# Sparse attention in one program with its projections: queries ahead of gates, probabilities scaled on GpSimd, two weight quarters on VectorE

## The chip, the core and the metric

The kernel runs on one core of a Trainium2 chip. The core has five engines with a queue of their own each: TensorE (PE, matmuls), VectorE (DVE), ScalarE (ACT), GpSimd (POOL) and SyncE (SP, which issues transfers). They run side by side and wait for each other by semaphores. The metric is the device time of one execution in microseconds (us); lower is better.

## What is computed

One inference step of a two-layer encoder for 1024 new frames ("prompt") and 32 frames of a running stream ("sample") with 512 cached positions. The first layer is a sparse attention, the second a gated linear recurrence; both have a SiLU gate and an output projection. The change is in the first layer:

```
p = rmsnorm(h) @ w_in                  # split into q, k, v, z (gate), qi, ki, wi (indexer)
q, k, qi, ki = rope(q), rope(k), rope(qi), rope(ki)
score = sum_h wi[h] * relu(qi[h] @ ki.T)          # 8 indexer heads
sel = top_k(score, n_sel)                         # 256 keys (prompt), 136 (sample)
logits = q @ k[sel].T * ATT_SCALE                 # 8 heads of 128, 2 key heads
probs = softmax(logits)                           # admissible selected keys only
o = probs @ v[sel]
out = (o * silu(z)) @ w_out
```

Tokens are handled in 9 tiles: 0 to 7 are 128 prompt tokens each, tile t sees 128(t + 1) keys; tile 8 is the sample (32 tokens, 544 keys). Tiles 0 and 1 need no selection.

## The kernel before

The kernel is four programs ("blocks") one after the other, with a barrier of all engines between them: `norm_and_project` (line 259), `attention` (line 878), `out_and_recur` and `final_out`. Inside a program each engine works through a fixed list of instructions.

**Projecting** (`attention_project`). All tokens are kept transposed, in three parts of 352 columns. The weights come in tiles of 128 columns in the order of `TILES` (line 48): the indexer key, eight indexer queries, two keys, then for each head the gate tile (Z) and the query tile (Q). A tile and a part make a "unit": 24 matmuls on TensorE (`product`, line 187; each value is split into a high and a low half and three products are summed), then for a query unit three copies on ScalarE (lines 667 to 672), three operations on GpSimd (lines 721, 724, 710) which rotate it, and a store by SP to the DRAM tensor `q_rotated` (line 547); for a gate unit one SiLU on ScalarE (line 675). TensorE may be up to four units ahead of ScalarE, which reads the banks. Between the units the weights are split by ScalarE (line 209) and GpSimd (line 216), and rotated keys are turned into rows (`rows_before`) and stored.

**The threshold search** (`search`, `count_signs`). The selection is found by 31 steps of bisection on the bits of a threshold. In each step VectorE proposes a value (line 802), counts scores above it for five of the seven tiles (line 793), while ScalarE counts for the two largest (line 651); then VectorE decides (lines 808, 809). The search runs beside the last 48 units (gates and queries). ScalarE does step n after a unit chosen by `counted_after`: units are put down as 3850 ns each and a step as `PACE`, 6000 ns.

**Attending** (`attention`). 72 items, one for each tile and head. For item i: TensorE multiplies queries by keys (line 941) into one of two halves of the PSUM tensor `wide`; VectorE adds the mask and takes the minimum (`shift`, line 1027); ScalarE takes the exponential and its sum (line 1067); two items later VectorE takes the reciprocal (line 1035) and scales the probabilities (`divide`, line 1037); TensorE transposes them (line 954) four items behind the multiplication, ScalarE copies them out of the banks (line 1077), TensorE mixes the values in groups of four heads (line 970), and VectorE multiplies by the gate (line 1043). The probabilities have a ring of 5 buffers, in the space of the normalised rows. In tiles 1 to 7 VectorE also makes the mask of tile t + 1, one of eight marking operations (lines 1003 to 1017) in each item between `shift` and `divide`. The queries come back from DRAM tile by tile (`q_tile`, line 913). In items 48 and 56 ScalarE splits the high half of one quarter of the output weights (line 194); GpSimd makes the low half (line 201). The other two quarters' low halves are made by VectorE in the next program.

## Time and profile before

| | us |
|---|---|
| median of 3 runs | 1458.36 (1457.74 to 1459.96) |
| the profiled execution | 1460.28 |
| its span in the profile | 1458.5 |
| TensorE busy in the span | 1382.0 (95%) |
| VectorE busy | 927.7 (64%) |
| ScalarE busy | 640.3 (44%) |
| GpSimd busy | 553.8 (38%) |
| granted TensorE clock, mean | 0.982 of full speed |

The span is the time from the first instruction to the last in the profile of one execution. Busy time of TensorE is modelled and counts matmuls that wait in its pipeline, so 95% does not mean 95% of the peak. The busy shares are averages over stages that are limited by different engines; the stages by time are: normalising and first units to 260 us, gates and queries with the search from 260 to 442 us, attending from 457 to 650 us, output projection and recurrence, final output.

### The profile page before, as it was taken

The page shows a single profiled execution, that of the slowest core. Times are in us where ns is not written, and L with a number is a line of the kernel's source. Part 1 is how long each engine was busy: PE and PEld are TensorE (multiplying, and loading weights), DVE is VectorE, ACT ScalarE, POOL GpSimd, SP SyncE. Part 2 cuts the span into 40 slices and gives each one's busy share as a digit, 9 for nine tenths or more (in the row PEclk, how much of TensorE's full clock was granted, in tenths as well). Part 3 has the DMA queues.
Part 4 walks back from the last instruction along what each step waited for, and adds up shares of the span by engine and source line. Part 5 has one row for each costly group of instructions (what it writes and reads, how often), then busy time and mean ns, then how long its engine had stood idle before and what let it go on. Part 6 is the DMA issues. An engine that isn't in the chain of part 4 may idle for free. (4 is left out here: it accounts for less than half of the span.)

```text
span 1458.5 us, 21147 instructions
## 1 busy us (share of the span) xinstructions
PE 1382.0 (95%) x8028; PEld 1204.3 (83%) x8028; DVE 927.7 (64%) x1702; ACT 640.3 (44%) x1123; POOL 553.8 (38%) x399
## 2 busy tenths in 40 slices
PE   5999999999995899999998999999999999997998
PEld 5999845999993455548888999999999999996786
DVE  4211287878887988744557676767585858596233
ACT  4333365667765555541124534343443435343121
POOL 2466600455641001100023655556464737373000
PEclk9999999999997999999999999999999999998999
DMA  7221100223211400002221101111111111105221
GB/s 217 91 56 44 44 1 1 65 81 99 71 40 59 159 15 19 0 30 84 90 78 46 44 25 55 36 44 35 44 35 45 35 44 35 45 6 209 101 87 65
DMA packets 95315, 86.80 MB, mean 60 GB/s; under 512 B 5584, under 2 KB 83280, under 8 KB 95216
## 3 DMA queue, kind: packets, MB, share of 16 engines
q1 hardware_dynamic: 93584, 80.63, 18.0%
q0 software_dynamic: 1632, 4.82, 0.9%
q8 instruction: 66, 1.08, 0.3%
q14 instruction: 33, 0.27, 0.1%
HBM read 65.46 MB, written 19.97 MB: 59 GB/s over the span
## 5 line engine op out<-in xcount | busy, mean ns | idle before, releaser
L187 PE MATMUL bank<-hn_hi,rw_hi 128*128 128x352 f32 x768 | 251.7, 328 | 1.6 <-DVE hn_lo L177 1.6
L187 PE MATMUL bank<-hn_hi,rw_lo 128*128 128x352 f32 x768 | 247.9, 323 | 0.0
L187 PE MATMUL bank<-hn_lo,rw_hi 128*128 128x352 f32 x768 | 247.6, 322 | 0.0
L187 PE MATMUL bank<-hn_hi,w_hi 128*128 128x352 f32 x648 | 209.9, 324 | 0.0
L187 PE MATMUL bank<-hn_lo,w_hi 128*128 128x352 f32 x648 | 207.8, 321 | 0.0
L187 PE MATMUL bank<-hn_hi,w_lo 128*128 128x352 f32 x648 | 207.7, 321 | 0.0
L187 PEld LDWEIGHTS bank<-hn_hi,rw_hi 128*128 128x128 f32 x768 | 145.1, 189 | 3.5 <-issue 3.0
L187 PEld LDWEIGHTS bank<-hn_lo,rw_hi 128*128 128x128 f32 x768 | 145.6, 190 | 0.0
L187 PEld LDWEIGHTS bank<-hn_hi,rw_lo 128*128 128x128 f32 x768 | 145.2, 189 | 0.0
L721 POOL TENSOR_TENSOR swapped<-swapped,sin 128x352 f32<-128x352 f32 x57 | 54.0, 947 | 190.8 <-ACT swapped L668 125.8
L187 PEld LDWEIGHTS bank<-hn_hi,w_hi 128*128 128x128 f32 x648 | 121.6, 188 | 0.5 <-ACT relu L682 0.5
L187 PEld LDWEIGHTS bank<-hn_lo,w_hi 128*128 128x128 f32 x648 | 121.8, 188 | 0.0
L187 PEld LDWEIGHTS bank<-hn_hi,w_lo 128*128 128x128 f32 x648 | 121.5, 187 | 0.0
L793 DVE TENSOR_SCALAR_CACHE_REDUCE marks<-score,bits 128x384 bf16<-128x384 f32 (+5 forms) x157 | 117.1, 805 | 1.1
L240 POOL TENSOR_SCALAR stats<-stats 128x1 f32<-128x1 f32 (+1 forms) x27 | 6.5, 241 | 280.0 <-ACT junk L1242 152.0
L1273 POOL TENSOR_TENSOR rw_lo<-rw_raw,rw_hi 128x1024 fp32r<-128x1024 f32 x32 | 95.3, 2982 | 35.8 <-ACT rw_hi L1266 35.7
L1471 PE MATMUL wide<-levels 128*128 128x128 f32 (+1 forms) x832 | 98.0, 273 | 1.2 <-DVE last_state L1785 1.1
L1471 PEld LDWEIGHTS wide<-levels 128*128 128x128 f32 (+1 forms) x832 | 92.5, 185 | 6.7 <-issue 1.9
L1067 ACT ACTIVATE probs<-probs,low 128x128 f32<-128x128 f32 (+8 forms) x72 | 55.6, 772 | 88.3 <-DVE low L1027 87.8
L941 PE MATMUL wide<-kT,q_tile 128*128 128x512 f32 (+3 forms) x192 | 75.7, 508 | 14.8 <-DMA q_tile<-q_rotated 14.8
L1639 POOL TENSOR_TENSOR levels<-levels,k_rec 128x528 f32<-128x528 f32 (+1 forms) x48 | 89.0, 1878 | 1.4 <-ACT levels L1557 1.4
L1749 DVE TENSOR_TENSOR levels<-levels,q_rec 128x528 f32<-128x528 f32 (+1 forms) x48 | 87.4, 1886 | 0.0
(230 smaller groups left out, 2926.1 us busy)
## 6 DMA issues: line engine op xcount, KB each, us to landing
rw_raw<-in_rec_w_in SPq DMA_DIRECT2D x32, 512.0 KB, 4.0
w_raw<-in_att_w_in SPq DMA_DIRECT2D x27, 512.0 KB, 4.0
q_rotated<-relu SPq DMA_DIRECT2D x24, 176.0 KB, 1.9
xin<-in_x_prompt SPq DMA_DIRECT2D x8, 512.0 KB, 3.8
q_tile<-q_rotated SPq DMA_DIRECT2D x8, 512.0 KB, 3.9
wo_raw<-in_att_w_out SPq DMA_DIRECT2D x4, 1024.0 KB, 9.2
x_again<-in_x_prompt SPq DMA_DIRECT2D x8, 512.0 KB, 4.1
residual<-h_rows SPq DMA_DIRECT2D x8, 512.0 KB, 2.9
```

The costliest lines, as they stand in the source:

```text
L187: last = pe.matmul(out, l, r, start=n == 0, stop=n == len(passes) - 1)
L240: pool.tensor_scalar(stats[0:r, 1, t:t + 1], stats[0:r, 0, t:t + 1], 1.0 / D, EPS, ALU.mult, ALU.add).then_inc(pool_order, 1)
L721: pool.tensor_tensor(swapped[:, r % 3, :], swapped[:, r % 3, :], sin[:, part * CW:(part + 1) * CW], ALU.mult).then_inc(sin_done, 1)
L793: step(dve.tensor_scalar(marks[0:r, i % 2, 0:keys(t)], tile(i, t), bound, 0.0, op, ALU.add, accum_out=counts[0:r, first + i:first + i + 1]))
L941: last = pe.matmul(logits[0:rows(t), i % 2, a:e], q[:, t % 2, h, 0:rows(t)], src[:, h // GROUP, a:e], start=True, stop=True)
L1067: act.activation(probs[0:r, i % RING, 0:n], probs[0:r, i % RING, 0:n], ACT.Exp, scale=-1.0, bias=low[0:r, 0, i:i + 1], accum_out=low[0:r, ...
L1273: pool.tensor_tensor(S["rw_lo"][:, slot], S["rw_raw"][:, slot], S["rw_hi"][:, slot].bitcast(F32), ALU.subtract).then_inc(S["rec_lo_done"], 1)
L1471: last = pe.matmul(out[:, 0:r], left, right, start=True, stop=True)
L1639: pool.tensor_tensor(x, x, level_view(k[:, slot], m)[:, :, 0, :], ALU.mult).then_inc(k_scaled, 1)
L1749: dve.tensor_tensor(x, x, level_view(q[:, slot], m)[:, :, 1, :], ALU.mult).then_inc(q_scaled, 1)
```

## The change

- `TILES`: for each head the query tile comes ahead of the gate tile, so that the last three units are gates.
- `PACE` is 5000 instead of 6000.
- `norm_and_project` and `attention` become one program, `project_and_attend`, without a barrier between them. What the barrier did is done by waits: VectorE waits ahead of the first `shift` for the last unit read by ScalarE and the last stored rows; TensorE waits ahead of the first item for the key rows and the cache, and ahead of its first transpose for the banks.
- The queries of tiles 0 and 1 go to a space of their own, `q_first`, over the tables of cosines and sines, so that they can be loaded once the last query is stored. Tiles 2 and up use `q_tile` as before; tile 2 waits for the first item.
- GpSimd scales the probabilities. VectorE keeps the reciprocal.
- The low halves of the first two output weight quarters are made by VectorE, at i = 52 and i = 60 of its loop.

```
 for _i in range(HEADS):
-    TILES += [Z0 + P * _i, Q0 + P * _i]
+    TILES += [Q0 + P * _i, Z0 + P * _i]
...
+        S["q_first"] = Space(nc, space.at)("q_first", [P, 2, HEADS, P])
         S["cos"] = space("cos", [P, T])
...
-    BITS, PACE = 31, 6000
+    BITS, PACE = 31, 5000
...
             for t in range(NT):
-                if t >= 2:
+                if t == 2:
+                    sp.wait_ge(logits_ready, 1)
+                elif t >= 4:
                     sp.wait_ge(logits_ready, HEADS * (t - 1))
-                sp.dma_start(q[:, t % 2, :, 0:rows(t)],
-                             q_dram[:, :, span(t)].rearrange("h p t -> p h t")).then_inc(q_in[t % 2], 16)
+                sp.dma_start(queries(t)[:, :, 0:rows(t)],
+                             q_dram[:, :, span(t)].rearrange("h p t -> p h t")).then_inc(
+                                 q_in_first[t] if t < 2 else q_in[t % 2], 16)
...
+        def gpsimd(pool):
+            def divide(i):
+                t, h = items[i]
+                r, n = rows(t), keys(t)
+                pool.wait_ge(inv_done, i + 1)
+                pool.tensor_scalar(probs[0:r, i % RING, 0:n], probs[0:r, i % RING, 0:n], low[0:r, 2, i:i + 1], None,
+                                   ALU.mult).then_inc(probs_ready, 1)
+
             pool.tensor_copy(kTs[:, :, PAST:], kT[:, :, SEQ:T]).then_inc(keys_done, 1)
-            for c in range(2):
-                out_weights_lo(pool, S, c)
+            for i in range(N):
+                divide(i)
...
+            pe.wait_ge(S["k_rows_out"], NT)
+            pe.wait_ge(S["cache_out"], 3)
             for i in range(N + LAG + 4):
+                if i == LAG:
+                    pe.wait_ge(*S["units_read"])
+                    pe.wait_ge(*S["ropes_read"])
...
+            dve.wait_ge(S["open_done"], 3)
+            dve.wait_ge(*S["units_read"])
+            S["rows_stored"](dve)
             for i in range(N + 12):
...
                 if 2 <= i <= N + 1:
-                    divide(i - 2)
+                    t, h = items[i - 2]
+                    dve.wait_ge(exp_done, i - 1)
+                    dve.reciprocal(low[0:rows(t), 2, i - 2:i - 1], low[0:rows(t), 1, i - 2:i - 1]).then_inc(inv_done, 1)
+                if i in (6 * HEADS + 4, 7 * HEADS + 4):
+                    out_weights_lo(dve, S, i // HEADS - 6)
```

Three places show the order of instructions. The first is SP's queue at the hand-over from projecting to attending (`q_rotated<-relu` is a store of a rotated query part, `q_tile` and `q_first` are query loads). Before:

```order
L547 DMA q_rotated<-relu 128x352 [waits rope_done] x6
L267 UNCONDITIONAL_BRANCH [waits stored0,v_stored,stored1,q_stored1,q_stored0]
L908 UNCONDITIONAL_BRANCH [waits barrier_Pool_Activation_PE_DVE_SP_release]
L913 DMA q_tile<-q_rotated 128x8x128 x2
L913 DMA q_tile<-q_rotated 128x8x128 [waits logits_ready] x2
L918 DMA wo_raw<-in_att_w_out 128x4x512 x4
```

After:

```order
L547 DMA q_rotated<-relu 128x352 [waits rope_done] x5
L928 DMA q_first<-q_rotated 128x8x128 [waits q_stored1,q_stored0]
L928 DMA q_first<-q_rotated 128x8x128
L928 DMA q_tile<-q_rotated 128x8x128 [waits logits_ready]
L928 DMA q_tile<-q_rotated 128x8x128
L935 DMA wo_raw<-in_att_w_out 128x4x512 [waits logits_ready]
```

The first two query loads now wait for the stored queries alone.

The second place is VectorE's list in tile 1, two items (the operation on `wide` is `shift`, `marks` and `score` belong to a marking operation). Before:

```order
L1027 ISA probs,low<-wide,open_mask 128x256 [waits pT_ready,logits_ready]
L1027 ISA low 128x1
L1010 TENSOR_SCALAR marks,counts<-score,select_state 128x384
L1035 RECIPROCAL low<-low 128x1 [waits exp_done,mark_order]
L1037 TENSOR_SCALAR probs<-probs,low 128x128 [waits inv_done]
L1027 ISA probs,low<-wide,open_mask 128x256 [waits pT_ready,logits_ready]
L1027 ISA low 128x1
L1012 TENSOR_SCALAR marks<-score,select_state 128x384
L1035 RECIPROCAL low<-low 128x1 [waits exp_done,mark_order]
L1037 TENSOR_SCALAR probs<-probs,low 128x256 [waits inv_done]
```

After:

```order
L1055 ISA probs,low<-wide,open_mask 128x256 [waits pT_ready,logits_ready]
L1055 ISA low 128x1
L1038 TENSOR_SCALAR marks,counts<-score,select_state 128x384
L1080 RECIPROCAL low<-low 128x1 [waits exp_done,mark_order]
L1055 ISA probs,low<-wide,open_mask 128x256 [waits pT_ready,logits_ready]
L1055 ISA low 128x1
L1040 TENSOR_SCALAR marks<-score,select_state 128x384
L1080 RECIPROCAL low<-low 128x1 [waits exp_done,mark_order]
```

The scaling behind each reciprocal has left VectorE's list; the next `shift` stands directly behind the reciprocal.

The third place is GpSimd's list in the attention. Before:

```order
L923 COPY kT_sample<-kT 128x2x32
L201 TENSOR_TENSOR wo_lo<-wo_raw,wo_hi_85 128x4x512 [waits wo_hi] x2
```

After:

```order
L948 COPY kT_sample<-kT 128x2x32
L945 TENSOR_SCALAR probs<-probs,low 128x128 [waits inv_done] x8
L945 TENSOR_SCALAR probs<-probs,low 128x256 [waits inv_done] x8
L945 TENSOR_SCALAR probs<-probs,low 128x384 [waits inv_done] x8
L945 TENSOR_SCALAR probs<-probs,low 128x512 [waits inv_done] x8
L945 TENSOR_SCALAR probs<-probs,low 128x640 [waits inv_done] x8
```

The two weight operations have left GpSimd's list and 72 scalings have come in (the rows go on to 1024 keys and the sample).

## Rows read from the trace of the kernel before

**Rows 1.** The head of the page: the span of the profiled execution.

```profile
span 1458.5 us, 21147 instructions
```

**Rows 2.** Stretches: length; busy us of PE, PEld, DVE, ACT, POOL; granted clock; DMA.

```profile
259.20:441.80 182.60, 182.54 (x1155) 182.00 (x1154) 151.16 (x400) 128.35 (x236) 96.38 (x83) 1.00 0.24 68
441.80:457.30 15.50, 0.81 (x4) 0.81 (x4) 9.28 (x32) 4.90 (x8) 4.22 (x6) 0.59 0.34 102
...
462.40:475.10 12.70, 10.34 (x34) 5.51 (x33) 11.17 (x45) 6.65 (x27) 0.00 (x0) 0.87 0.21 58
475.10:489.90 14.80, 12.53 (x45) 6.28 (x45) 14.14 (x47) 8.14 (x25) 0.00 (x0) 1.00 0.94 336
489.90:507.00 17.10, 15.95 (x59) 8.44 (x59) 16.44 (x46) 9.69 (x25) 0.00 (x0) 1.00 0.08 21
507.00:528.40 21.40, 19.90 (x83) 11.86 (x84) 19.36 (x47) 12.14 (x29) 0.00 (x0) 1.00 0.11 31
528.40:553.20 24.80, 24.47 (x99) 13.92 (x98) 21.93 (x46) 13.76 (x32) 0.00 (x0) 1.00 0.09 26
553.20:584.20 31.00, 28.67 (x110) 15.65 (x109) 27.08 (x45) 17.27 (x33) 4.53 (x1) 1.00 0.04 6
584.20:616.80 32.60, 31.81 (x120) 16.77 (x118) 25.87 (x45) 18.30 (x32) 4.53 (x1) 1.00 0.00 0
```

**Rows 3.** Timelines of PE and DVE at the hand-over: start, length, instruction, [idle before].

```profile
441.42 0.32 PE L187 MATMUL bank<-hn_hi,w_lo 128*128 128x352 f32 x1
...
451.81 0.17 DVE L834 COPY_PREDICATED bits<-bits 128x7 uint32<-128x7 uint32 x1
...
456.50 3.17 PE L941 MATMUL wide<-kT,q_tile 128*128 128x128 f32 x10 [14.75 <-DMA q_tile<-q_rotated]
...
457.33 0.29 DVE L1027 CUSTOM_DVE_ANT_0 probs<-wide,open_mask 128x128 f32<-128x128 f32 x1 [5.35 <-PE wide L941]
```

**Rows 4.** Line 547, the last ten stores: issue ns min/median/max, first and last start.

```profile
L547 SPq DMA_DIRECT2D q_rotated<-relu x10: 319/320/345, 379.7 to 448.2; - x10
```

**Rows 5.** The page's DMA issues: KB each, us from issue to landing.

```profile
q_rotated<-relu SPq DMA_DIRECT2D x24, 176.0 KB, 1.9
...
q_tile<-q_rotated SPq DMA_DIRECT2D x8, 512.0 KB, 3.9
```

**Rows 6.** Timeline of DVE, the start of two steps of the search.

```profile
263.22 0.16 DVE L802 TENSOR_SCALAR bits<-bits 128x7 uint32<-128x7 uint32 x1
...
267.63 0.17 DVE L802 TENSOR_SCALAR bits<-bits 128x7 uint32<-128x7 uint32 x1
```

**Rows 7.** Groups by line, 263 to 452 us: busy us, mean ns, idle before.

```profile
L808 DVE TENSOR_TENSOR bits<-counts,select_state 128x7 uint32<-128x7 f32 x31 | 14.4, 466 | 28.6 <-ACT signs L651 28.0
...
L809 DVE COPY_PREDICATED bits<-bits 128x7 uint32<-128x7 uint32 x31 | 12.6, 407 | 1.1
...
L802 DVE TENSOR_SCALAR bits<-bits 128x7 uint32<-128x7 uint32 x31 | 11.1, 358 | 1.0
```

**Rows 8.** Groups by line and form on DVE, 455 to 652 us.

```profile
L1037 DVE TENSOR_SCALAR probs<-probs,low 128x1024 f32<-128x1024 f32 x8 | 6.0, 753 | 0.3
...
L1027 DVE CUSTOM_DVE_ANT_0 probs<-wide,score 128x384 f32<-128x384 f32 x8 | 4.4, 549 | 0.0
...
L1037 DVE TENSOR_SCALAR probs<-probs,low 128x384 f32<-128x384 f32 x8 | 3.4, 420 | 0.3
```

**Rows 9.** Lines 1615 (GpSimd) and 201 (VectorE): duration ns min/median/max.

```profile
L1615 POOL TENSOR_SCALAR k_rec<-k_rec x8: 1063/1067/1103, 782.3 to 1257.8; 128x1056 f32<-128x1056 f32 x8
...
L201 DVE TENSOR_TENSOR wo_lo<-wo_raw,wo_hi x2: 2282/2286/2291, 653.2 to 655.4; 128x2048 fp32r<-128x2048 f32 x2
```

**Rows 10.** Timelines of POOL and DVE around the second weight quarter.

```profile
589.45 4.53 POOL L201 TENSOR_TENSOR wo_lo<-wo_raw,wo_hi 128x2048 fp32r<-128x2048 f32 x1 [26.86 <-ACT wo_hi L194]
...
590.57 3.90 DVE L1037 TENSOR_SCALAR probs<-probs,low 128x896 f32<-128x896 f32 x1
594.39 1.21 DVE L1027 CUSTOM_DVE_ANT_0 probs<-wide,score 128x1024 f32<-128x1024 f32 x1
```

More of the change, by code:

```diff
@@ L155, in build @@
         S["tables_in"], S["cache_in"] = sem("tables_in"), sem("cache_in")
-        norm_and_project(nc, S, space)
-        attention(nc, S)
+        project_and_attend(nc, S, space)
         out_and_recur(nc, S)
@@ L256, in cached_keys, with project_and_attend @@
     return score[:, 0:PAST // P * 384].rearrange("p (b c) -> p b c", b=PAST // P)
-def norm_and_project(nc, S, space):
+def project_and_attend(nc, S, space):
     swapped = space("swapped", [P, 3, CW])
@@ L265, in norm_and_project @@
     S["swapped"], S["relu"] = swapped, relu
-    first, later = input_norm(nc, S), attention_project(nc, S)
+    stages = [input_norm(nc, S), attention_project(nc, S), attention(nc, S)]
     with nc.Block() as block:
@@ L269, in _ @@
         def _(sp):
-            first["sync"](sp)
-            later["sync"](sp)
+            for stage in stages:
+                stage["sync"](sp)
         @block.tensor
         def _(pe):
-            first["tensor"](pe)
-            later["tensor"](pe)
+            for stage in stages:
+                stage["tensor"](pe)
         @block.scalar
         def _(act):
-            first["scalar"](act)
-            later["scalar"](act)
+            for stage in stages:
+                stage["scalar"](act)
         @block.gpsimd
         def _(pool):
-            first["gpsimd"](pool)
-            later["gpsimd"](pool)
+            for stage in stages:
+                stage["gpsimd"](pool)
         @block.vector
         def _(dve):
-            first["vector"](dve)
-            later["vector"](dve)
+            for stage in stages:
+                stage["vector"](dve)
 def input_norm(nc, S):
@@ L940, in multiply @@
                     e = min(n, a + 512)
-                    last = pe.matmul(logits[0:rows(t), i % 2, a:e], q[:, t % 2, h, 0:rows(t)],
+                    last = pe.matmul(logits[0:rows(t), i % 2, a:e], queries(t)[:, h, 0:rows(t)],
                                      src[:, h // GROUP, a:e], start=True, stop=True)
@@ L1029, in shift @@
                                          op1=ALU.min, accum_out=low[0:r, 0, i:i + 1]).then_inc(logits_read, 1)
-            def divide(i):
-                t, h = items[i]
-                r, n = rows(t), keys(t)
-                dve.wait_ge(exp_done, i + 1)
-                dve.reciprocal(low[0:r, 2, i:i + 1], low[0:r, 1, i:i + 1]).then_inc(inv_done, 1)
-                dve.wait_ge(inv_done, i + 1)
-                dve.tensor_scalar(probs[0:r, i % RING, 0:n], probs[0:r, i % RING, 0:n], low[0:r, 2, i:i + 1], None,
-                                  ALU.mult).then_inc(probs_ready, 1)
             def gate(g):
@@ L1055, in _, with scalar @@
                 if 2 <= i <= N + 1:
-                    divide(i - 2)
+                    t, h = items[i - 2]
[3 more added lines that the diff above has]
+                    out_weights_lo(dve, S, i // HEADS - 6)
                 if i >= 12 and i % 4 == 0:
                     gate((i - 12) // 4)
-        @block.scalar
-        def _(act):
+        def scalar(act):
             for i in range(N + LAG):
@@ L1082, in _ @@
                     out_weights_hi(act, S, i // HEADS - 6)
+    return dict(sync=sync, tensor=tensor, scalar=scalar, gpsimd=gpsimd, vector=vector)
 def out_and_recur(nc, S):
```

40 lines of the change are left out of this document (24 added, 16 removed).

## The prediction

> **What bounds the kernel now.** I read the page's head first: the profiled execution spans 1458.5 us [rows 1] and the run it belongs to took 1460.28 us, so 1.8 us lie around the span; the median of the runs shown is 1458.36 us. I take the saving off the span and then off the median. The page's chain of waits covers only the last 110 us and says nothing about the stage that is changed, so I went on to the table of stretches [rows 2], cut where the first score read (line 1027) of each query tile starts. It shows four regimes. Until 441.8 us TensorE is busy 182.54 of 182.60 us: the projections are bound by TensorE. Then follows a hole of 15.5 us in which TensorE does 0.81 us of work. In tiles 1 to 3 (462.4 to 507.0) VectorE is the busier engine: 14.14 of 14.80 us in tile 2, 16.44 of 17.10 in tile 3, against 12.53 and 15.95 for TensorE, whose figure is generous because it counts the overlapping ends of matmuls. From tile 7 on TensorE is the bound again, 31.81 of 32.60 us. So the change can win in two places: the hole, and the tiles in which VectorE is the slower one. Everything after 650 us is the same code, behind the same barrier.
>
> **The hand-over, part by part.** The hole before has three members in series [rows 3]. The last projection matmul ends at 441.42 + 0.32 = 441.7 (call it T). VectorE ends the threshold search only at 451.81 + 0.17 = 452.0. Then comes the barrier between the two programs, then the query load, and TensorE's first score matmul starts at 456.50, its reader on VectorE at 457.33. T to that reader is 15.6 us. The change acts on each member.
>
> The search: 31 steps, and step n must be answered by ScalarE, which does its share at fixed places among its 48 last projection units. Before, a step is scheduled every 6.0 us of units, after, every 5.0 us. A step takes VectorE 267.63 - 263.22 = 4.4 us undisturbed [rows 6]. The three small operations that close and open it are held at times: their means are 0.466, 0.407 and 0.358 us against 0.17 undisturbed [rows 7], 0.30 + 0.24 + 0.19 = 0.7 us a step. So VectorE needs 5.1 us a step, 31 x 5.1 = 158 us, and from 263.2 it could be through at 421. With some waiting left I take 430, 12 us before T. The search then no longer ends last.
>
> What is late next is the query load. The stores of the rotated queries must land before SP may load them. Before, the last query unit is also the last unit: its store is issued at 448.2 [rows 4], 6.5 us after T, and lands 1.9 us later [rows 5], at T + 8.4. After, three gate units stand behind it; 182.6 us over 48 units are 3.8 us each, 11.4 us in all. The store lands at T - 3.0, the load is issued at once and takes 3.9 us [rows 5]: queries at T + 0.9. From first matmul to first reader were 0.83 us [rows 3] at a granted clock of 0.59; I take 0.7. First reader at T + 1.6 instead of T + 15.6: **14.0 us saved**. The bounds: if the two loads delay each other and ScalarE is late with its first exponential, 12; if the queries are there in time and only the last gate holds VectorE, 15. Moving queries ahead of gates costs nothing in the projections themselves: the same 48 units in another order, and TensorE has no gap there whose cover could go. SP's queue is moved too: the two loads now stand behind the last row stores of the keys, which are some 17 units earlier, and the next two tile loads wait for the first score, since their space is that of the normalised rows.
>
> **The scaling on GpSimd.** Removed from VectorE are 72 operations at line 1037, 0.42 us for 384 keys and 0.753 for 1024 [rows 8]; the next operation starts 0.08 us before such a one ends (594.39 against 590.57 + 3.90 in [rows 10]), so the relief is 0.34 us at 384 keys and 0.067 us more or less for each 128: 0.27, 0.34 and 0.41 us an item in tiles 1, 2 and 3, or 2.2, 2.7 and 3.3 us a tile of 8. The trace has no such operation on GpSimd. The nearest row is its one-source multiply-add over 128x1056, 1.067 us [rows 9], about 1.0 ns an element: 0.4, 0.5 and 0.6 us for these tiles, and 1.1 us at 1024, four times less than the 4.1 us an item that tile 7 takes. The upper bound is its two-source subtraction, 4.53 us for 2048 elements [rows 10], 2.3 us at 1024; even that fits. I take the one-source row, since the new operation reads one tensor and a scalar. GpSimd is otherwise empty here (one operation of 4.53 us in each of tiles 6 and 7 [rows 2]). The result is needed two items later, so its own length and one semaphore hop more are hidden by that distance.
>
> What is not hidden is that the two engines get in each other's way. While GpSimd runs its subtraction from 589.45 to 593.98, a scaling of 896 keys on VectorE, which needs less than the 0.753 us of 1024, lasts 3.90 us and ends 0.5 us behind it [rows 8, 10]. So VectorE's marking operations (one an item in tiles 1 to 7) may be held by a scaling that GpSimd is still doing. Between the reciprocal that starts the scaling and the marking operation stands the score read, 0.549 us at 384 keys [rows 8], one source of it in PSUM, against about 0.5 us of scaling, plus the start: 0.1 us is left over an item, 0.8 us a tile. The bounds are nothing, and the whole scaling (0.5 us an item, 4 us a tile), if the score read is held too. The Trainium skill, "GPSIMD Engine Reference", 1. Specifications, says that the SBUF interfaces are shared with VectorE, with contention from VectorE instructions in a 2-port mode or with two SBUF inputs; the score read is neither. By that rule the small end holds, and the trace agrees in the one 3.90 us row. The same page, 4.1 Engine selection, speaks against the change: GpSimd is about half as fast for two-input elementwise work, and roughly at line rate for one input.
>
> Tile by tile. TensorE's own work in a tile's stretch goes by 2t + 1 (scores of tile t, half the transposes of t and of t - 1, mixing of t - 1), so from 31.8 us in tile 7 [rows 2] it is 2.12 x (2t + 1): 6.4, 10.6, 14.8, 19.1, 23.3 and 27.6 us in tiles 1 to 6. Before, against these: 12.7, 14.8, 17.1, 21.4, 24.8, 31.0. After:
> tile 1: 12.7 - 2.2 + 0.6 = 11.1 (VectorE); tile 2: 14.8 - 2.7 + 0.8 = 12.9 (VectorE); tile 3: VectorE 17.1 - 3.3 + 0.8 = 14.6, TensorE 14.8, and two equal bounds do not mesh, 16.0; tile 4: 19.1 plus 1.0 for the same reason, 20.1; tile 5: 24.2; tiles 7 and 8 as now, tile 0 too (it goes by ScalarE's exponentials as much as by VectorE). That is 1.6 + 1.9 + 1.1 + 1.3 + 0.6 = 6.5 us.
>
> **The two weight quarters.** In tile 6 TensorE loses 31.0 - 27.6 = 3.4 us, the most of all tiles; there GpSimd's first quarter holds VectorE, and a second one does so in tile 7 [rows 10]. They go to VectorE at 2.286 us each [rows 9], into items whose VectorE sum leaves about 1.2 us free. Each thus makes one score read late by 1 to 2 us, of which TensorE feels about half. Held 3.2 us twice before, late 1 to 2 us twice after: 1.9 us saved, between -1 and 3.5.
>
> **Sum.** 14.0 + 6.5 + 1.9 = 22.4 us. Span 1458.5 - 22.4 = 1436.1; against the median, 1458.4 - 22.4 = **1436 us**.
>
> **The rivals.** (A) GpSimd holds VectorE for the whole scaling in every item. Then in tiles 1 to 3 the relief of 8.2 us is paid back with 3.2, 4.0 and 4.8 us, tiles 4 to 6 stay as they are, and only the hand-over is won: 1458.4 - 14.0 + 3.8 = 1448, or 1443 if half of the items are held. For it: the 3.90 us row. Against it: the score read between. Chance 0.12. (B) The coupling of three engines costs more today than I allow, and after the change every tile goes at its own bound: 6.4 does not bind in tile 1 (VectorE 10.5), but 12.1, 14.8, 19.1, 23.3 and 27.6 do. That is 2.2 + 2.7 + 2.3 + 2.3 + 1.5 + 3.4 = 14.4 us in the stage instead of 8.4, 1430, and with the better end of the hand-over 1429. Chance 0.12. (C) The other side: the faster schedule of the search. ScalarE takes its units in order; if a step cannot keep to 5.0 us, ScalarE falls behind and, three units (11.4 us) behind, TensorE stands still in a stretch where it has no idle time at all. Behind by 4 + 31 x (s - 4.96) for steps of s; it cancels 22.4 us at 34 us behind, s = 5.9. Today a step lasts 188.8 / 31 = 6.1 us; were that inherent, 38 us behind, 27 us lost: 1463. Against it: my 5.1 us are 1.0 below today's, and the rest is waiting for the slow schedule. ScalarE is busy 128.35 of 182.6 us [rows 2], so it has room for the denser counts; stepping through the first 33 units with these lengths I found it at most 7 us behind. Chance 0.04. (D) The hand-over fails in part: the query chain (stores, then loads) takes 6 to 10 us longer than counted, or the change does not move the search ahead: 1442 to 1450. Chance 0.06.
>
> **How the numbers follow.** Forecast 0.66 (1432 to 1441), A 0.12, B 0.12, C 0.04, D 0.06. The range must take in B's 1429 and most of A, so 1429 to 1446; it leaves out C, half of D and the worse end of A, some 0.15. A measurement of this kernel can tell about 0.2% (2.9 us) from no change; only C reaches there, with a sliver of D: faster 0.95, same 0.02, slower 0.03.
>
> **What would show it.** In the profile after, the last bit operation of the search should end near 430, before the last projection matmul; TensorE's hole should be about 1 us and wait for the query load; the new GpSimd operations should measure about 1.0 ns an element; a marking operation should show 0.1 us of holding, not 0.5; tile 1 should take 11 us and tile 6 29. ScalarE's counts should start behind their units by single microseconds. I am wrong if TensorE has gaps before the hand-over (C), if the stage from first score read to last gate is still above 190 us (A), or below 180 (B).

## The result, and the profile after

| | before | after |
|---|---|---|
| median, us | 1458.85 (4 runs, 1457.74 to 1459.96) | 1448.12 (4 runs, 1446.90 to 1449.22) |
| ratio after / before | | 0.9926, 95% interval 0.9914 to 0.9938 |
| profiled execution, its span | 1460.28, 1458.5 | 1447.48, 1445.6 |

The change makes the kernel 10.7 us faster, not 22.4; 1448.1 is above the range's upper end of 1446. One run among all those below, 2304.02 us at a granted clock of 0.56 (PACE 5500 with early additions), is left out. In the profiled executions the spans differ by 12.9 us, and that can be laid out by place: the first score read comes at 450.6 instead of 457.3 (6.7 us), from there to the last gate of the sample ("the stage" below) it takes 187.0 instead of 192.4 us (5.4 us), and the rest 808.0 instead of 808.8. So the hand-over gave half of the 14.0 that it should, and the stage 5.4 of 8.4.

The stretches of after, with the columns of [rows 2]. The first is the hole at the hand-over, then come tiles 1 to 7 and the sample:

```profile
445.85:450.60 4.75, 0.99 (x5) 0.93 (x4) 0.00 (x1) 1.75 (x2) 0.00 (x0) 0.73 0.83 221
...
455.83:466.48 10.65, 8.03 (x32) 4.27 (x31) 9.37 (x36) 6.43 (x26) 6.14 (x8) 1.00 0.06 8
466.48:479.10 12.62, 12.06 (x44) 5.95 (x44) 11.54 (x38) 8.02 (x26) 9.23 (x10) 1.00 0.89 331
479.10:495.60 16.50, 16.30 (x61) 8.62 (x62) 14.05 (x38) 9.87 (x26) 11.50 (x8) 1.00 0.12 34
495.60:516.42 20.82, 20.14 (x85) 11.86 (x84) 15.63 (x38) 12.20 (x29) 15.52 (x9) 1.00 0.15 42
516.42:540.78 24.36, 24.36 (x98) 13.92 (x97) 18.36 (x38) 13.76 (x32) 16.22 (x9) 1.00 0.09 26
540.78:571.30 30.52, 28.61 (x110) 15.70 (x109) 22.16 (x38) 17.26 (x33) 21.87 (x9) 1.00 0.03 6
571.30:602.99 31.69, 31.66 (x120) 16.66 (x118) 19.01 (x37) 18.27 (x32) 23.33 (x9) 1.00 0.00 1
...
602.99:637.62 34.63, 33.31 (x152) 17.12 (x152) 8.64 (x30) 13.42 (x42) 20.66 (x11) 0.97 0.01 1
```

Three things are to be seen. VectorE is no longer the busier engine in tiles 2 and 3 (14.05 of 16.50 us in tile 3, before 16.44 of 17.10); in tile 1 it still is, 9.37 of 10.65 us against TensorE's 8.03. The fifth busy column, GpSimd, was to be near 5 us in tile 3 and is 11.50; in tile 7 it is 23.33. And tile 6 has hardly moved (30.52 against 31.0), while the sample, 33.0 us long before (616.8 to the last gate at 649.7), has become longer.

The hand-over, timelines of TensorE, VectorE, ScalarE, GpSimd and SP with the columns of [rows 3]:

```profile
415.84 0.43 PE L187 MATMUL bank<-hn_hi,w_hi 128*128 128x352 f32 x1 [0.86 <-ACT relu L676]
...
421.63 0.43 PE L187 MATMUL bank<-hn_hi,w_hi 128*128 128x352 f32 x1 [1.67 <-ACT relu L676]
...
426.54 0.43 PE L187 MATMUL bank<-hn_hi,w_hi 128*128 128x352 f32 x1 [0.79 <-ACT qiT_zT_gT L679]
...
436.27 0.64 DVE L838 COPY_PREDICATED bits<-bits 128x7 uint32<-128x7 uint32 x1
...
439.42 0.45 ACT L676 COPY relu<-bank 128x352 f32<-128x352 f32 x1 [4.03 <-DMA q_rotated<-relu]
...
441.76 1.84 POOL L714 TENSOR_TENSOR relu<-relu,swapped 128x352 f32<-128x352 f32 x2
...
445.54 1.00 SPq L928 DMA_DIRECT2D q_first<-q_rotated  x2
...
445.57 0.32 PE L187 MATMUL bank<-hn_hi,w_lo 128*128 128x352 f32 x1
...
449.65 2.53 PE L965 MATMUL wide<-kT,q_first 128*128 128x128 f32 x8 [3.76 <-DMA q_first<-q_rotated]
...
450.60 0.29 DVE L1055 CUSTOM_DVE_ANT_0 probs<-wide,open_mask 128x128 f32<-128x128 f32 x1 [13.69 <-PE wide L965]
```

The search is indeed out of the way (436.9). But TensorE, which before had no gap there, now waits three times for ScalarE, and T, the end of the last projection matmul, is at 445.9 instead of 441.7. The queries are rotated and stored late as well, so that their loads start at 445.5 and TensorE waits 3.76 us for them. The 14.0 us saved were reckoned from T to the first reader, 15.6 down to 1.6. It is 450.60 - 445.89 = 4.7, and T itself has slipped by 4.2: 15.6 - 4.7 - 4.2 = 6.7.

### The profile page after: what moved, and what is told of

The parts are those of the page before. It is cut to its first block and busy times, and to the rows that moved or that the text cites. A ratio compares the mean times of both kernels' runs of the same rounds, so it can differ in the third digit from the quotient of the medians.

```text
span 1445.6 us, 21141 instructions
## 1 busy us (share of the span) xinstructions
PE 1380.3 (95%) x8028; PEld 1202.4 (83%) x8028; DVE 904.1 (63%) x1632; ACT 641.2 (44%) x1123; POOL 674.3 (47%) x469
## 5 line engine op out<-in xcount | busy, mean ns | idle before, releaser
L945 POOL TENSOR_SCALAR probs<-probs,low 128x128 f32<-128x128 f32 (+8 forms) x72 | 127.7, 1778 | 62.8 <-DVE low L1080 62.6
```

The costliest lines, as they stand in the source:

```text
L945: pool.tensor_scalar(probs[0:r, i % RING, 0:n], probs[0:r, i % RING, 0:n], low[0:r, 2, i:i + 1], None, ALU.mult).then_inc(probs_ready, 1)
```

## Theory and rivals

My theory after the traces had three parts. (1) The hand-over lost 7.3 us because PACE 5000 asks for a search step every 5.0 us and VectorE needs 5.5, so that ScalarE, which answers the steps in order with its units, comes late. That is rival C's mechanism at a fraction of its size. The rivals: it is the order of the units, or the joined program. (2) GpSimd's scaling is 2.5 times slower than its own multiply-add, by the pointer operand or by the one-operation form, or because VectorE is in its way. (3) The weight quarters cost time on VectorE, by where they stand or wherever they stand.

The experiments ran on three chips. Each was compared with runs of the kernel before on its own chip, whose medians were 1462.0 us (the runs with gates first, PACE 5500, VectorE's scaling, a constant), 1459.8 us (PACE 6000, early additions, two operations, quarters one item earlier) and 1458.2 us (the others). So the ratios, not the times, compare the experiments with each other and with the 0.9926 of the changed kernel; where the intervals of two ratios overlap, the argument rests on the stretches of the profiled executions.

## Experiments on the hand-over

**Gates ahead of queries again**, all else as changed.

```
-    TILES += [Q0 + P * _i, Z0 + P * _i]
+    TILES += [Z0 + P * _i, Q0 + P * _i]
```

> The changed kernel with the gate tile ahead of the query tile again. Theory (the order takes 11.4 us of the query chain out of the hand-over): the last store is issued 6.5 us behind the last projection matmul, queries arrive 10 to 11 us behind it, first score read near 453 to 456; total 3 to 6 us above 1448. Rival (the order brings nothing, since ScalarE and GpSimd are late with the last query tile either way): total within 1 us.

Measured: 1457.72 us (1455.47 to 1459.29), ratio 0.9970 (0.9958 to 0.9982); the first read is at 457.72, where it was before the change at 457.33 [rows 3], and later than the 453 to 456 that I expected: the order is worth more than I thought.

```profile
452.67 1.00 SPq L928 DMA_DIRECT2D q_first<-q_rotated  x2
...
456.77 3.36 PE L965 MATMUL wide<-kT,q_first 128*128 128x128 f32 x10 [12.41 <-DMA q_first<-q_rotated]
```

The search ends at 438.0 here and does not matter: stores and loads of the queries alone fill the whole hole. Joining the programs and hurrying the search bring nothing at all at the hand-over without the new order. What is left of the gain is the stage.

**Order and pace alone**, in the kernel before: two programs, old place of the queries, scaling and quarters as before. The edit is against the kernel before.

```
-    TILES += [Z0 + P * _i, Q0 + P * _i]
+    TILES += [Q0 + P * _i, Z0 + P * _i]
-    BITS, PACE = 31, 6000
+    BITS, PACE = 31, 5500
```

> The kernel before with only two numbers changed: queries ahead of gates, and PACE 5500. The two programs stay apart, the barrier and the old place of the queries stay, scaling and quarters too. Search and stores then end no later than in the joined kernel with PACE 5500 (search at 443.4, last store at 439.8 plus landing), so the barrier falls near 444 to 445 and the load is issued behind it: first read at 450 to 452 us, 5.5 to 7 us better than before, and that is also the gain of the total (ratio 0.9955). Rival (joining is what brings the gain; order and pace alone move nothing, since the barrier and both chains still stand in series behind the last unit): first read at 455 to 457, ratio 0.999 to 1.0.

Measured: 1452.09 us (1451.53 to 1453.10), ratio 0.9956 (0.9942 to 0.9969), the first read at 448.70, 8.6 us earlier than before and 1.9 us earlier than in the changed kernel. That is better than the 450 to 452 expected, and the rival, that only the joined program brings the gain, has fallen. Order and pace did it together; the order with PACE 6000 in two programs was not run:

```profile
443.36 0.17 DVE L834 COPY_PREDICATED bits<-bits 128x7 uint32<-128x7 uint32 x1
...
444.02 9.18 SPq L913 DMA_DIRECT2D q_tile<-q_rotated  x3
...
447.87 3.17 PE L941 MATMUL wide<-kT,q_tile 128*128 128x128 f32 x10 [7.27 <-DMA q_tile<-q_rotated]
```

From the end of the search to the load behind the barrier it is 0.5 us (444.02 against 443.53). The barrier was never dear; what stood in front of it was. Two changed numbers give more at the hand-over than the joined program with PACE 5000. At the same pace of 5500 the joined program, below, issues the load at 441.73 and reads at 446.94, so joining is worth 1.8 us.

**PACE 6000**, all else as changed (`BITS, PACE = 31, 6000`).

> The changed kernel with PACE back at 6000. Pace theory (the search needs 5.5 us a step, so 5000 makes ScalarE late and 5500 does not; 6000 puts the last count behind the units): TensorE has no gap before the hand-over (T near 441), but the search ends near 452 and the first score read is at 452.5 to 453.5, since it waits on VectorE: 2 to 3 us later than with 5000. Ratio 0.994 to 0.995. Rival (the end of the search is hidden whatever its pace, only the query chain counts): first read at 447, ratio 0.990.

Measured: 1449.37 us (1448.17 to 1450.16), ratio 0.9928 (0.9916 to 0.9940). TensorE has no gap up to T = 440.9, and VectorE is the last to be ready, as the pace theory has it. The place was wrong by 3 us: the first read is at 449.19, since the search ends at 449.0 and not at 452. So the total is that of the changed kernel, where I expected 2 to 3 us more (ratio 0.994 to 0.995).

```profile
448.86 0.17 DVE L838 COPY_PREDICATED bits<-bits 128x7 uint32<-128x7 uint32 x1
449.19 0.29 DVE L1055 CUSTOM_DVE_ANT_0 probs<-wide,open_mask 128x128 f32<-128x128 f32 x1 [0.15 <-DVE bits L838]
```

ScalarE starts its last count at 441.36; in the kernel before, where the last unit is a query with three copies and a wait for a slot, at 444.43. That is the 3 us.

**PACE 5500**, all else as changed.

> The changed kernel with the search scheduled at 5.5 us a step in place of 5.0. Theory 1 (a step really takes 5.5 us, ScalarE falls behind the schedule, TensorE waits 3.3 us for it and the last query unit is late): no waits of TensorE for ScalarE ahead of the hand-over, the last projection matmul ends near 442 in place of 445.8, first score read near 445; total about 1443. Theory 2 (the lateness comes from the queries' own chain, copy, rotation, store, load): the last projection matmul moves, the first score read stays near 450; total 1447 or more.

Measured: 1448.69 us (1447.16 to 1450.15), ratio 0.9904 (0.9890 to 0.9919). TensorE has no gap up to T = 440.7, the search ends at 443.6, and the first read is at 446.94, 3.7 us earlier than in the changed kernel and 2 us later than expected. The pace thus explains half of the 7.3 us that I had put down to it. The hole now waits for the queries alone:

```profile
435.63 0.45 ACT L676 COPY relu<-bank 128x352 f32<-128x352 f32 x1 [3.78 <-DMA q_rotated<-relu]
...
437.96 1.85 POOL L714 TENSOR_TENSOR relu<-relu,swapped 128x352 f32<-128x352 f32 x2
...
441.73 0.99 SPq L928 DMA_DIRECT2D q_first<-q_rotated  x2
...
445.99 3.35 PE L965 MATMUL wide<-kT,q_first 128*128 128x128 f32 x10 [5.25 <-DMA q_first<-q_rotated]
```

The first row is a wait that I had not priced: the copy of the last query part needs one of two `relu` slots, and the slot is held until GpSimd has added the sine part to an earlier unit and SP has stored it. GpSimd adds one unit late (`add_sine` runs behind the next unit's products); the two last additions stand together at the end.

**PACE 5500 and early additions**: for the last three query units GpSimd adds at once.

```
                 pending.append((i, r, rotated(i)))
+                if kind == "q" and n_q[i] >= n_q[N] - 3:
+                    add_sine()
```

> PACE 5500, and for the last three query units GpSimd adds the sine part at once instead of one unit later. Slot theory (the last store is late because ScalarE's copy waits 3.8 us for a relu slot that the delayed addition still holds): with PACE 5500 alone the first score read was at 446.9 us; here the 3.8 us wait is gone, the last additions end near 437 instead of 439.8, the first read is at 443.5 to 444.5, and the kernel takes about 1445.5 (before at about 1459 on the same chip: ratio 0.990 - 0.002 = 0.988). Rival (the chain is GpSimd's own work, and the addition only changes places): first read stays within 1 us of 446.9, ratio 0.990.

Measured: 1442.86 us (1442.24 to 1443.19), ratio 0.9884 (0.9869 to 0.9899). The 3.8 us wait is gone, the last addition ends at 437.6, the loads start at 439.51 and the first read is at 444.16, as expected: 13.2 us earlier than before, T + 2.6.

**One-source operations on GpSimd**, PACE 5000. It asks why a step takes 5.5 us. Only query units are changed, and the kernel leaves out their rotation.

```
-                pool.tensor_tensor(swapped[...], swapped[...], sin[...], ALU.mult).then_inc(sin_done, 1)
+                pool.tensor_scalar(swapped[...], swapped[...], 1.0, 0.0, ALU.mult, ALU.add).then_inc(sin_done, 1)
...
-                pool.tensor_tensor(rotated(i), rotated(i), cos[...], ALU.mult).then_inc(cos_done, 1)
+                pool.tensor_scalar(rotated(i), rotated(i), 1.0, 0.0, ALU.mult, ALU.add).then_inc(cos_done, 1)
...
-                pool.tensor_tensor(dst, dst, swapped[...], ALU.add).then_inc(rope_done, 1)
+                pool.tensor_scalar(dst, dst, 1.0, 0.0, ALU.mult, ALU.add).then_inc(rope_done, 1)
```

> The changed kernel (PACE 5000), in which GpSimd passes the queries on by three one-source operations in place of its three two-source ones, so the rotation of the queries is left out; the weights' low halves stay two-source. Hold theory (the three small operations of a search step lose 0.98 us a step because GpSimd's two-source operations hold them): the loss falls to 0.2 to 0.5 us, a step takes 4.6 to 4.9 us instead of 5.5, ScalarE keeps up, TensorE has no gap before the hand-over (T near 441 instead of 445.9), and the first read is at 443 to 445 instead of 450.6; ratio 0.9926 - 0.0045 = 0.988. Rival (the step is inherently 5.5 us, by semaphores and ScalarE's counts): step 5.3 us or more, TensorE's 3.3 us of gaps stay, first read at 448 or later.

Measured: 1439.40 us (1438.73 to 1441.07), ratio 0.9872 (0.9857 to 0.9887). The three small operations of a step, groups by line as in [rows 7], first in after, then here:

```profile
L813 DVE COPY_PREDICATED bits<-bits 128x7 uint32<-128x7 uint32 x31 | 23.2, 747 | 1.1
...
L806 DVE TENSOR_SCALAR bits<-bits 128x7 uint32<-128x7 uint32 x31 | 13.6, 440 | 1.0
...
L812 DVE TENSOR_TENSOR bits<-counts,select_state 128x7 uint32<-128x7 f32 x31 | 9.5, 306 | 4.4 <-ACT signs L655 3.0 <-DVE marks L797 0.4
```

```profile
L819 DVE COPY_PREDICATED bits<-bits 128x7 uint32<-128x7 uint32 x31 | 10.9, 353 | 1.1
...
L812 DVE TENSOR_SCALAR bits<-bits 128x7 uint32<-128x7 uint32 x31 | 6.5, 209 | 1.0
...
L818 DVE TENSOR_TENSOR bits<-counts,select_state 128x7 uint32<-128x7 f32 x31 | 5.9, 191 | 15.3 <-ACT signs L655 14.6
```

At 0.17 us undisturbed they lose 0.58 + 0.27 + 0.14 = 0.98 us a step in after, and 0.24 here. With that TensorE has no gap (T = 441.0), the search ends at 423.2, and the first read is at 441.74, T + 0.7, better than expected. The steps start 5.1 us apart, not 4.6 to 4.9, because VectorE now waits for ScalarE's counts (14.6 us in the last row). The hold is the cause of the loss in a step; whether the second source or the longer time of GpSimd's operations does it, the run does not part. It can be watched in after, VectorE and GpSimd at the same moment:

```profile
340.75 0.92 DVE L806 TENSOR_SCALAR bits<-bits 128x7 uint32<-128x7 uint32 x1
```

```profile
340.70 0.95 POOL L725 TENSOR_TENSOR swapped<-swapped,sin 128x352 f32<-128x352 f32 x1 [1.86 <-ACT relu L676]
```

A 0.17 us operation starts 0.05 us behind GpSimd's and ends with it. The Trainium skill, "SBUF — State Buffer", Who interferes with whom, says that of VectorE in a 2-port mode and GpSimd "Whoever issues first gets the shared pair for the whole instruction"; these rows agree, though no row tells in which mode the small operation runs. Part of the 8.9 us that the first read gains here against after comes from GpSimd's own operations, 0.49 us each instead of 0.95, which shorten the query chain; the runs do not part the two shares. The three gaps of TensorE are the search's share, since they went with PACE 5500 alone.

## Experiments on the scaling

**VectorE scales**, quarters and hand-over as changed.

```
                     dve.reciprocal(...).then_inc(inv_done, 1)
+                    dve.wait_ge(inv_done, i - 1)
+                    dve.tensor_scalar(probs[...], probs[...], low[0:rows(t), 2, i - 2:i - 1], None, ALU.mult).then_inc(probs_ready, 1)
...
-            for i in range(N):
-                divide(i)
```

> The changed kernel with the scaling of the probabilities back on VectorE; all else as changed. Theory 1 (the scaling on GpSimd gives the attending stage 5 of the 12 us won, by relieving VectorE in tiles 1 to 3): the stage from first score read to last gate goes from 187.3 back to about 192 us, tile 1 from 10.65 back to 12.7, tile 2 from 12.6 to 14.7; total about 1453 us against 1448. Theory 2 (GpSimd is so slow here, 2.5 to 3.0 ns an element, that it gives nothing; what shortened the stage is the end of GpSimd's weight quarters): tiles 6 and 7 stay short, total within 2 us of 1448.

Measured: 1457.53 us (1455.32 to 1458.16), ratio 0.9963 (0.9949 to 0.9977). The stage is 194.2 us (449.96 to 644.12), 7.1 more than in after (192 was expected), so the scaling on GpSimd brings 7.1 us even at its real price. By tiles: 5.4 us in tiles 1 to 5, 3.1 in tiles 6 and 7, 0.3 in tile 0, and 1.7 lost in the sample. Theory 2 has fallen. The stage is also 1.8 us more than before (192.4), though the scaling is the same. That lies in tile 6, 32.9 us long where it was 31.0, but it is not all a price of the first quarter on VectorE at i = 52 (a wait of TensorE, and a stretch with the columns of [rows 2]):

```profile
569.51 1.73 PE L976 MATMUL bank<-ident,probs 128*128 128x128 f32 x7 [2.64 <-ACT pT L1103]
...
569.50:574.50 5.00, 4.99 (x14) 3.01 (x15) 3.34 (x6) 2.23 (x5) 0.00 (x0) 0.67 0.00 0
```

TensorE's wait is 2.64 us where it was 1.80 in the kernel before, and in the 5 us behind it the granted clock is 0.67, where tile 6 of before has 1.00 throughout. Some 0.8 us are the longer wait, and I estimate that the other 1.0 goes with the clock.

**A constant in place of the pointer**: `low[0:r, 2, i:i + 1]` becomes `0.01`.

> The changed kernel with GpSimd's scaling by a constant in place of the reciprocal read per row (the probabilities are not normalised, so outputs differ). Theory 1 (the scalar read from memory makes the GpSimd operation slow): 128x1024 falls from 3.09 to about 1.0 us, waits of TensorE for GpSimd (14 us of weight loads, 3.3 us of matmuls) vanish, the stage shortens by 2 to 4 us. Theory 2 (the operation is slow because ScalarE and VectorE use the memory at the same time): it stays at 2.5 to 3 us for 1024.

Measured: 1449.07 us (1448.36 to 1450.42), ratio 0.9908 (0.9893 to 0.9923); 128x1024 takes 3.015 us in the mean instead of 3.092. The pointer costs 0.07 us and is not the cause.

**Two operations in one instruction**: multiply, then add 0.0.

```
-                                   low[0:r, 2, i:i + 1], None, ALU.mult).then_inc(probs_ready, 1)
+                                   low[0:r, 2, i:i + 1], 0.0, ALU.mult, ALU.add).then_inc(probs_ready, 1)
```

> The changed kernel with GpSimd's scaling written as a multiplication and an addition of 0.0 in one instruction, as its multiply-add over 128x1056 at 1.07 us is. Form theory (the one-operation form is the slow one): 128x1024 takes 1.0 to 1.2 us instead of 3.09, TensorE's 17 us of waits for scaled probabilities go and the stage is 2 to 4 us shorter, ratio 0.990. Rival (the slowness is of this place or of a second scalar that is no constant): 3.0 to 3.3 us, same total as the changed kernel, ratio 0.9926.

Measured: 1445.91 us (1445.04 to 1447.65), ratio 0.9907 (0.9893 to 0.9921). Groups by form on GpSimd, in after and here:

```profile
L945 POOL TENSOR_SCALAR probs<-probs,low 128x1024 f32<-128x1024 f32 x8 | 24.7, 3092 | 6.0 <-DVE low L1080 6.0
...
L945 POOL TENSOR_SCALAR probs<-probs,low 128x384 f32<-128x384 f32 x8 | 10.0, 1254 | 3.4 <-DVE low L1080 3.4
```

```profile
L945 POOL TENSOR_SCALAR probs<-probs,low 128x1024 f32<-128x1024 f32 x8 | 10.9, 1365 | 19.6 <-DVE low L1080 19.6
...
L945 POOL TENSOR_SCALAR probs<-probs,low 128x384 f32<-128x384 f32 x8 | 4.7, 586 | 8.3 <-DVE low L1080 8.3
```

The form theory holds: the instruction that does more is 2.3 times faster in the mean. Undisturbed it is 1.12 us at 1024, the price that I had assumed, and the one-operation form is 2.85 us (both means have one scaling in them that VectorE's quarter holds). So neither the place nor VectorE beside it made it slow. The mean of 1.365 has one of 3.08 us in it, beside VectorE's quarter (timelines of GpSimd and VectorE):

```profile
584.63 1.12 POOL L945 TENSOR_SCALAR probs<-probs,low 128x1024 f32<-128x1024 f32 x1 [2.74 <-DVE low L1080]
589.10 3.08 POOL L945 TENSOR_SCALAR probs<-probs,low 128x1024 f32<-128x1024 f32 x1 [3.35 <-DVE low L1080]
```

```profile
588.93 2.27 DVE L201 TENSOR_TENSOR wo_lo<-wo_raw,wo_hi 128x2048 fp32r<-128x2048 f32 x1
```

The stage is 184.8 us, 2.2 less than after. Most of that, 1.7, is the sample, 32.96 us instead of 34.63:

```profile
634.39 0.46 PE L978 MATMUL bank<-ident,probs 32*128 32x32 f32 x5 [0.74 <-POOL probs L945]
...
634.30:637.60 3.30, 3.11 (x17) 2.40 (x17) 0.29 (x1) 0.33 (x2) 0.03 (x1) 0.72 0.03 5
```

Both rows are of after. TensorE waits for a scaling, and in the 3.3 us behind that the granted clock is 0.72, a mean of its two levels of 1.2 and 2.4 GHz, where the whole sample tile has 1.00 with the two-operation form. With the one-operation form the sample took 33.85, 34.63 and 35.42 us at clocks of 1.00 (one-source run), 0.97 (after) and 0.94 (early additions): the waits cost 0.9 us, the clock up to 1.6 more. What lowers the clock is not shown. With PACE 5500 the same wait stands in the same place, and the clock of that tile is 1.00:

```profile
630.80 0.46 PE L978 MATMUL bank<-ident,probs 32*128 32x32 f32 x5 [0.74 <-POOL probs L945]
```

With order and pace alone, where VectorE scales, TensorE has no wait there, and the last 2.3 us of the sample are at 0.52. In tile 5 (24.36 us in both) the form changes nothing, since TensorE binds there.

## Experiments on the quarters

**One item earlier**: i = 51 and 59 instead of 52 and 60.

```
-                if i in (6 * HEADS + 4, 7 * HEADS + 4):
+                if i in (6 * HEADS + 3, 7 * HEADS + 3):
```

> The changed kernel with the two weight quarters on VectorE at i = 51 and 59 instead of 52 and 60. Stacking theory (the 2.3 us subtraction falls into the item whose score read was already held by GpSimd, and into the one with a gate): the TensorE gap of 1.9 us near 563.8 goes, tile 6 is 29 to 29.5 us instead of 30.5, stage 1.5 to 2 us shorter. Rival (2.3 us more on VectorE cost TensorE the same wherever they stand): tile 6 30.3 to 30.7, no change in the total.

Measured: 1445.82 us (1445.54 to 1447.33), ratio 0.9908 (0.9893 to 0.9924). Tile 6 is 28.77 us instead of 30.52, tiles 1 to 5 stay within 0.03; the stage is 185.6 us, 1.4 shorter. The rival has fallen. In after the quarter stands behind the longest marking operation and ahead of a gate:

```profile
555.68 2.29 DVE L1042 TENSOR_TENSOR_SCAN ranks<-marks 128x1024 f32<-128x1024 bf16 x1
...
558.08 2.27 DVE L201 TENSOR_TENSOR wo_lo<-wo_raw,wo_hi 128x2048 fp32r<-128x2048 f32 x1
560.27 0.68 DVE L1062 TENSOR_TENSOR qiT_zT_gT<-bank,qiT_zT_gT 128x512 f32<-128x512 f32 x1
560.87 1.08 DVE L1055 CUSTOM_DVE_ANT_0 probs<-wide,score 128x896 f32<-128x896 f32 x1
```

```profile
563.75 0.96 PE L978 MATMUL bank<-ident,probs 128*128 128x128 f32 x7 [1.91 <-ACT pT L1102]
```

5.2 us of other work part two score reads, and TensorE's ring of two halves is too short for that. One item earlier the same 2.27 us fall beside a marking operation of 0.15 us, and TensorE's largest gap in that stretch is 0.15 us.

**The quarters back on GpSimd**, behind the scalings of items 47 and 55.

```
             for i in range(N):
                 divide(i)
+                if i in (6 * HEADS - 1, 7 * HEADS - 1):
+                    out_weights_lo(pool, S, i // HEADS - 5)
...
-                if i in (6 * HEADS + 4, 7 * HEADS + 4):
-                    out_weights_lo(dve, S, i // HEADS - 6)
```

> The changed kernel with the two weight quarters back on GpSimd, in its queue behind the scalings of items 47 and 55. Theory (the move to VectorE cost about 1.8 us, since the kernel with VectorE's scalings and quarters needs 194.2 us for the stage and the one before 192.4): the stage is 185 to 186 us, ratio 0.9915. Rival (with scalings of 3 us on GpSimd its queue has no room for 4.5 us more, so that the scalings behind the quarter come 4 to 5 us late and TensorE waits): stage 188 to 191, ratio 0.994.

Measured: 1448.85 us (1448.02 to 1451.31), ratio 0.9936 (0.9923 to 0.9948), stage 189.0 us. My theory fell and its rival held. GpSimd's queue, from the timeline:

```profile
549.19 4.96 POOL L201 TENSOR_TENSOR wo_lo<-wo_raw,wo_hi 128x2048 fp32r<-128x2048 f32 x1
554.14 8.43 POOL L945 TENSOR_SCALAR probs<-probs,low 128x896 f32<-128x896 f32 x3
```

Three scalings come late behind the quarter, and TensorE waits 2.31 us for the first. Tiles 6 and 7 together take 63.8 us, in after 62.2, and with the quarters one item earlier 60.4; the ratio does not part the first two. So the 1.8 us lost belong to a VectorE that also scales, and in part to the clock; with the scalings on GpSimd the quarters are better on VectorE, above all one item earlier.

## All of it together

PACE 5500, early additions, quarters at i = 51 and 59, two operations.

> All that helped, together: PACE 5500, the sine part added at once for the last three query units, the quarters at i = 51 and 59, GpSimd's scaling in the two-operation form. If the effects add, the first read stays at 444.2 us, the stage from there to the last gate is 182.5 to 183.5 us (187.0 in the changed kernel, less 2.2 for the form and 1.7 for the place of the quarters), and the ratio is about 0.985. If form and place mend the same waits of TensorE, the stage is 184.8 and the ratio 0.987.

Measured: **1437.62 us** (1436.41 to 1440.07), ratio 0.9858 (0.9844 to 0.9871), 20.6 us faster than the kernel before on the same chip. First read at 444.03, stage 183.5 us (to 627.54): the effects add. It beats both kernels. TensorE still waits 2.17 us for the first queries, and 1.9 us in all for scaled probabilities.

The hand-over of all kernels, from their timelines (us):

| kernel | T | search ends | first query load issued | first read |
|---|---|---|---|---|
| before (PACE 6000) | 441.7 | 452.0 | 452.5 | 457.3 |
| gates first, PACE 5000 | 444.4 | 438.0 | 452.7 | 457.7 |
| after (PACE 5000) | 445.9 | 436.9 | 445.5 | 450.6 |
| PACE 6000 | 440.9 | 449.0 | 437.9 | 449.2 |
| order and pace alone (5500) | 440.6 | 443.5 | 444.0 | 448.7 |
| PACE 5500 | 440.7 | 443.6 | 441.7 | 446.9 |
| PACE 5500, early additions | 441.5 | 441.8 | 439.5 | 444.2 |
| one-source GpSimd, PACE 5000 | 441.0 | 423.2 | 435.1 | 441.7 |

The first read follows the last of three: T, the end of the search, and the issue of the load plus 4.6 to 5.2 us. In the last row that is T, with 0.7 us more; with PACE 6000 it is the search.

## Why the prediction was wrong

**What bounds the kernel**: right. The time came from the hole and from the tiles in which VectorE was the slower one.

**The search, 5.1 us a step**: this step failed first. In after the steps start at 263.2 to 427.7, 164.5 / 30 = 5.5 us apart. I had taken the holding of the three small operations, 0.7 us a step, from the slow schedule [rows 7]. The same work of GpSimd falls on denser steps, and the loss is 0.98 us. So the search ended at 436.9 and not at 430, harmless in itself, but ScalarE waited 31.6 us for VectorE's proposals (8.1 before), and three times passed that on to TensorE. I had stepped through only the first 33 units; the gaps lie at 415 to 427, behind them. This is C, to which I gave 27 us at 6.1 us a step; at 5.5 us its own formula gives 4 + 31 x 0.52 - 11.4, almost 9 us, and T slipped by 4.2. (At 6.1 us the formula gives 39 us behind and not 38.) I treated it as an all-or-nothing case, and left no share of it in the sum.

**The query chain**: this step failed too, by 3.1 us. "The store lands at T - 3.0" took the gate units as the only thing that moves; the last store was issued at 443.6 and landed at about T - 0.4, the loads landed at T + 3.8. The row that I lacked was ScalarE's wait for a `relu` slot, 4.03 us here. The trace of before had it, in ScalarE's timeline, and I passed over it since it was small:

```profile
444.07 0.45 ACT L672 COPY relu<-bank 128x352 f32<-128x352 f32 x1 [1.34 <-DMA q_rotated<-relu]
```

With the pace at 5500 and the additions at once T + 2.6 was reached, and with short GpSimd operations T + 0.7, against my T + 1.6: the mechanism was right, the sum lacked two resources. D (6 to 10 us, chance 0.06) named the chain, but not this cause.

**The scaling, 6.5 us**: the sum came near, on a wrong price and partly by luck. It was a sum over tiles 1 to 5, which gained 5.8 us in after and 5.4 by the experiment; that the experiment gives 7.1 in all comes from tiles 6 and 7, where I had expected nothing of the scaling, less the sample. In tile 1 the clock helped as well: with VectorE's scaling it takes 12.7 us at 0.87 in before, but 12.0 at 1.00 with order and pace alone. The 12.7 that I started from held up to 0.7 us of low clock, and after has 1.00 there. GpSimd needs 1.25 and 3.09 us at 384 and 1024 keys in the mean, where I had taken the one-source row of 1.07 us for 1056 and called 2.3 us at 1024 the upper bound. Both are exceeded, and "roughly at line rate for one input" holds of the two-operation form alone. It did little harm because the two items of distance hide 3 us in tile 7 as well (31.7 us with either form); the harm is where that distance is short in time, in the sample (1.7 us), for which I had written "as now". The holding was over-priced in tiles 1 and 2, which came to 10.65 and 12.62 us for 11.1 and 12.9. Rival A is refuted: VectorE's score read stays as before (0.556 us at 384 keys for 0.549), and only marking operations that fall into a scaling are held, the largest 1.306 us instead of 0.741. Rival B comes near in tile 1 alone (its bounds were 10.5 and 12.1 us); tiles 3 and 4 came to 16.50 and 20.82 us, above even my 16.0 and 20.1.

**The quarters, 1.9 us**: mis-sized. Tiles 6 and 7 together are 1.4 us shorter in after, with the relief by the scaling in it; the quarters alone, on a VectorE that scales, lost 1.8 us, of which some 1.0 goes with the clock, and moved from GpSimd to VectorE with the scalings on GpSimd they gain 1.6. "Items whose VectorE sum leaves about 1.2 us free" was true of the mean item, not of i = 52, where the 2.29 us marking operation and a gate are neighbours. At i = 51 tile 6 takes 28.8 us, which is what I had forecast for it (29).

**In sum**: 14.0 + 6.5 + 1.9 became 6.7 and 5.4 in the profiled execution. The 7.3 us missing at the hand-over are the 4.2 by which T slipped and the 3.1 of the query chain. The 3.0 missing in the stage are 1.7 in the sample, 0.7 in tiles 1 to 5, 0.5 in tiles 6 and 7 and 0.2 in tile 0. The combined kernel gives 20.6 us, but with four edits that the forecast did not know, so the forecast was near what could be won and wrong on how near this change comes to it. The marks that I gave do tell: the gaps of TensorE point to C, and GpSimd's 2.5 to 3 ns an element to the wrong row.

## What to carry to other kernels

When a schedule is tightened, take the length of its step with the disturbances that it will meet at the new density, and test the neighbourhood of the chosen number: here 5000, 5500 and 6000 bound in three different resources. Follow a hand-over through every slot and every delayed helper operation of its chain, since a wait that is small before is small only because something else ended later. Put a lump of work where the neighbouring items of that very place are short, not where the mean item is; and price an instruction by a row of the same form, or measure its form first.

## What the runs showed of the hardware

- GpSimd's TENSOR_SCALAR on 128x1024 float32 in SBUF takes 2.85 us with one operation and 1.12 us with two (multiply, add 0.0), undisturbed. With a constant in place of the pointer the one-operation form takes 2.77 us.
- Two-source GpSimd operations (0.95 us at 128x352) stretch 0.17 us operations of VectorE to up to 0.92 us, those with one source too; VectorE's two-source quarter in its turn stretches a 1.12 us scaling of GpSimd to 3.08 us.
- The granted clock fell to 0.72 over the 3.3 us behind a 0.74 us wait of TensorE, late in a stretch at 1.00. Behind the same wait it stayed at 1.00 in two other runs, and in one it fell to 0.52 with no wait ahead of it.
- The barrier between two programs took 0.5 us from the end of the last operation to the first load behind it.
